# Turned copies of the tokens from the host, split at once; the reciprocal root mean square applied behind the input projection

## The reference, cut to what matters

```python
def rms_norm(x, w):
    y = x * lax.rsqrt(jnp.mean(x * x, axis=-1, keepdims=True) + NORM_EPS)
    return y * w

h = rms_norm(x, norm1_w)                  # 512 x 1024
y = jnp.einsum("bsd,dn->bsn", h, w_in)    # w_in 1024 x 3852
fq, fk, fv, ff, rq, rk, rv, rg, gq, gk, gv, gz, ga, gb = split_columns(y)
qkv = concat([gq, gk, gv])                # 3 x 512 columns
qkv = silu(causal_depthwise_conv(qkv, gdn_conv_w))     # 4 taps along the tokens
# then: attention with forget gates (f*), retention (r*), gated delta rule (g*), w_out,
# a second norm, routed experts, a last norm
```

## Time and profile before

| what | us |
|---|---|
| median of 3 runs | 621.25 (620.01 to 622.05) |
| the profiled execution, its own time | 619.92 |
| its span in the trace | 618.0 |
| PE busy | 579.1 (94% of the span) |
| DVE / ACT / POOL busy | 245.6 / 198.6 / 179.8 |
| first matmul of the projection | at 11.78 |
| first matmul of granule 4 (group v0) | at 37.91 |
| first matmul of granule 16 (group rq) | at 109.99 |

### The profile page before, as it was taken

One profiled execution on the slowest core, in us unless ns is written; L12 is line 12 of the kernel. 1 busy time (PEld: TensorE's weight loads), 2 busy tenths in 40 slices (PEclk: granted clock), 3 DMA queues, 4 the chain that ended last, 5 costly groups with the idle time before them and its releaser, 6 DMA issues.

```text
span 618.0 us, 12011 instructions
## 1 busy us (share of the span) xinstructions
PE 579.1 (94%) x4922; PEld 446.4 (72%) x4922; DVE 245.6 (40%) x618; ACT 198.6 (32%) x429; POOL 179.8 (29%) x118
## 2 busy tenths in 40 slices
PE   7999999999999999999899999999999999987892
PEld 5987887799999888856679998666555565654440
DVE  6135553592216711287732146323332233321117
ACT  7344544523324261634635321111111121111113
POOL 1443434173268422421433301111112111120014
PEclk9999999999999999999999999999999999999997
DMA  9665443422121122003788878999999999999975
GB/s 338 202 187 157 146 134 97 134 70 51 56 70 36 37 69 70 1 2 122 271 325 305 318 265 313 357 421 423 428 422 427 423 429 423 423 425 428 419 299 229
DMA packets 44857, 150.63 MB, mean 244 GB/s; under 512 B 8552, under 2 KB 29760, under 8 KB 38274
## 3 DMA queue, kind: packets, MB, share of 16 engines
q1 hardware_dynamic: 40208, 141.67, 60.4%
q0 software_dynamic: 4528, 8.15, 3.6%
q10 hardware_dynamic: 66, 0.03, 0.0%
HBM read 141.69 MB, written 16.27 MB: 256 GB/s over the span
## 4 chain that ended last, share of the span: by engine, by line
PE 62%; DMA 19%; DVE 11%; issue 4%; ACT 2%; POOL 1%; SPq 0%; DVEq 0%; POOLq 0%; ACTq 0%
PE bank L772 29%; PE bank L796 9%; DMA xg<-h2d,tok 8%; DMA w<-in_expert_w_dram 8%; PE bank L1184 5%; PE bank L1138 4%; PE bank L1160 3%; PE bank L1084 2%; PE bank L1098 2%; DMA yd<-oy,dst 2%; DMA yt<-yd 1%; DVE Dm L1801 1%; PE bank L1078 1%; PE bank L1054 1%; DMA raw<-in_w_in_dram 1%
## 5 line engine op out<-in xcount | busy, mean ns | idle before, releaser
L1506 POOL TENSOR_TENSOR wlo<-raw,whi 128x1024 fp32r<-128x1024 f32 (+1 forms) x25 | 59.9, 2400 | 95.7 <-ACT whi L1207 95.7
L772 PE MATMUL bank<-wlo,hHi 128*128 128x256 f32 (+2 forms) x224 | 64.9, 290 | 0.0
L1138 PE MATMUL bank<-w,xT 128*64 128x256 f32 x512 | 58.2, 380 | 5.1 <-issue 5.1
L772 PE MATMUL bank<-whi,hHi 128*128 128x256 f32 (+1 forms) x208 | 59.9, 288 | 3.2 <-DVE cacc L1701 1.4
L1611 POOL DMA_INDIRECT yd<-oy,dst x15 | 15.1, 1009 | 162.7 <-DVE oy L2140 162.7
L1160 PE MATMUL bank<-w,xT 128*64 128x256 f32 x512 | 58.2, 380 | 2.6 <-DMA w<-in_expert_w_dram 2.6
L1184 PE MATMUL bank<-w,hidT 128*64 128x512 f32 x256 | 58.5, 599 | 1.1 <-ACT hidT L1483 1.1
L1138 PEld LDWEIGHTS bank<-w,xT 128*64 128x64 f32 x512 | 37.8, 137 | 29.4 <-issue 14.5
L772 PE MATMUL bank<-whi,hLo 128*128 128x256 f32 (+1 forms) x208 | 58.7, 282 | 0.0
L1160 PEld LDWEIGHTS bank<-w,xT 128*64 128x64 f32 x512 | 36.4, 137 | 21.5 <-DMA w<-in_expert_w_dram 3.5
L2123 DVE SCALAR_TENSOR_TENSOR hid<-bank,slot,sa 128x256 f32<-128x256 f32 x16 | 10.8, 676 | 94.6 <-issue 92.1
(11 more groups left out here) (374 smaller groups left out, 1121.2 us busy)
## 6 DMA issues: line engine op xcount, KB each, us to landing
w<-in_expert_w_dram SPq DMA_DIRECT2D x44, 2048.0 KB, 21.5
raw<-in_w_in_dram SPq DMA_DIRECT2D x24, 512.0 KB, 3.9
w<-in_expert_w_dram SPq DMA_DIRECT2D x8, 1024.0 KB, 7.1
yd<-zt SPq DMA_DIRECT2D x8, 512.0 KB, 5.1
yt<-yd SPq DMA_DIRECT2D x4, 1024.0 KB, 9.0
raw<-in_w_in_dram SPq DMA_DIRECT2D x6, 520.0 KB, 7.2
X<-in_x_dram SPq DMA_DIRECT2D x4, 512.0 KB, 5.8
raw<-in_w_out_dram SPq DMA_DIRECT2D x4, 512.0 KB, 3.3
```

What stands on the lines that cost most here:

```text
L772: m = pe.matmul(o, l, r, start=(at == 0 and c == 0 and i == 0), stop=(at == parts - 1 and kc == chunks[-1] and i == 2), skip_group_check=True)
L1138: m = pe.matmul(pb[3][r, 0:FF], xT[:, c, r], w1[u % 4][:, e, c * FF:(c + 1) * FF], start=(c == 0), stop=(c == KC - 1), skip_group_check=True)
L1506: pool.tensor_tensor(low_of(g), raw_of(g), high_of(g).bitcast(F32), ALU.subtract).then_inc(wlo_done, 1)
```

## The change

The host sends, beside x, a turned copy of it (`turned`, 128 partitions by 8 chunks by 512 tokens) and one small table `lead` with the norm's weights and the convolution's taps, both laid out by partition. The turned tokens are split at once: ScalarE's high part is a copy with the norm's weight as its scale, chunk by chunk (8 operations of 128x512), VectorE's low part multiplies and subtracts in one operation per chunk. The reciprocal root mean square is taken beside this (ScalarE squares tiles 0 and 1, VectorE tiles 2 and 3) and applied to the projection's outputs: as ScalarE's scale in the "n" groups, and in the "t" groups as a product with `RB`, a table of it along the tokens, which a new task "rb" behind granule 3 makes with four matmuls on TensorE and a copy on VectorE. In the convolution VectorE writes this product into a buffer `yr` in SBUF, which releases the bank; all four taps then read `yr`. fq and fk are evacuated by VectorE instead of ScalarE. TensorE no longer turns tokens; it runs 36 matmuls on zeros first, and runs granule 0 chunk by chunk over four open tiles. The low part of granule 0's weights is shared between VectorE and GpSimd.

```diff
-            tokens(0)
-            tokens(1)
-            sp.dma_start(CT[:, 0:NSTAY], consts[:, 0:NSTAY]).then_inc(s_const, 16)
+            def turned_tokens(i):
+                sp.dma_start(xt0[:, 2 * i:2 * i + 2, :].rearrange("p c n -> p (c n)"),
+                             turned[:, 2 * i * S:(2 * i + 2) * S]).then_inc(s_xt[min(i, 2)], 16)
...
             granule(0)
-            for t in range(2, T):
-                tokens(t)
-            for g in (1, 2):
-                granule(g)
-            sp.dma_start(CT[:, NSTAY:], consts[:, NSTAY:]).then_inc(s_const2, 16)
+            turned_tokens(0)
+            turned_tokens(1)
+            granule(1)
+            turned_tokens(2)
+            turned_tokens(3)
+            tokens(0)
+            tokens(1)
+            granule(2)
+            tokens(2)
+            tokens(3)
+            sp.dma_start(CT[:, 0:NSTAY], consts[:, 0:NSTAY]).then_inc(s_const, 16)
+            sp.dma_start(CT[:, NSTAY:], consts[:, NSTAY:]).then_inc(s_const, 16)
...
+            def first_granule():
+                n, _, _, chunks, _, w, _ = GRANULES[0]
+                hi, lo = high_of(0), low_of(0)
+                tiles = [begin(("y", n, b)) for b in range(T)]
+                pe.wait_ge(first_low, 1)
+                for c, kc in enumerate(chunks):
+                    pe.wait_ge(xlo_done, kc + 1)
+                    if c == HK // 2:
+                        pe.wait_ge(wlo_done, 1)
+                    for b in range(T):
...
+                if k[0] == "rb":
+                    pe.wait_ge(s_const, 32)
+                    pe.wait_ge(ssx_done, 3)
+                    four(k, lambda t, o: mm(o, rx[:, t:t + 1].broadcast_to([P, P]), ident))
...
+            zb = zt.bitcast(BF16)
+            pe.wait_ge(zero_set, 1)
+            for _ in range(WARM):
+                pe.matmul(pb[7][:, 0:256], zb[:, 0:P], zb[:, 0:256], start=True, stop=True)
...
+            def high_part(c):
+                act.wait_ge(s_xt[min(c // 2, 2)], 16 if c < HK else 32)
+                act.activation(hHi[:, c, :], xt0[:, c, :], ACT.Copy, scale=n1p[:, c:c + 1]).then_inc(hhi_done, 1)
+            weight_high(act, 0)
+            act.wait_ge(s_lead, 16)
+            for c in range(HK):
+                high_part(c)
+            weight_high(act, 1)
+            for c in range(HK, KC):
+                high_part(c)
             squares(0)
             squares(1)
...
+            weight_high(act, 2)
+            act.wait_ge(ssx_done, 1)
+            act.activation(ssx, ssx, ACT.Sqrt, scale=1.0 / D, bias=epsm[:, :]).then_inc(ssx_done, 1)
+            act.wait_ge(ssx_done, 3)
...
-                        cp = lambda dst, src: act.activation(dst, src, ACT.Copy)
+                        cp = lambda dst, src: act.activation(dst, src, ACT.Copy, scale=rx[:, t:t + 1])
...
-                        wait_full(act, name)
+                        act.wait_ge(conv_step, 2 * i + 1)
                         if i >= 2:
                             act.wait_ge(silu_done, i - 1)
-                        act.activation(cacc[i % 2][:, :], psum(name)[:, :], ACT.Copy,
+                        act.activation(cacc[i % 2][:, :], yr[i % 2][:, :], ACT.Copy,
                                        scale=PCW[:, 3, blk:blk + 1]).then_inc(tap0_done, 1)
                     for b in range(2):
                         i = CONVN[what] + b
-                        wait_read(act, ("y", n, b))
+                        act.wait_ge(conv_step, 2 * i + 2)
...
+            hc = slice(0, HK // 2)
+            dve.tensor_tensor(low_of(0)[:, hc, :], raw_of(0)[:, hc, :], high_of(0)[:, hc, :].bitcast(F32),
+                              ALU.subtract).then_inc(first_low, 1)
+            for c in range(KC):
+                dve.wait_ge(hhi_done, c + 1)
+                dve.scalar_tensor_tensor(out=hLo[:, c, :], in0=xt0[:, c, :], scalar=n1p[:, c:c + 1],
+                                         in1=hHi[:, c, :].bitcast(F32), op0=ALU.mult, op1=ALU.subtract).then_inc(xlo_done, 1)
+            for t in (2, 3):
+                dve.wait_ge(s_x[t], 16)
+                j = dve.tensor_tensor_reduce(out=X0[:, t, :], in0=X0[:, t, :], in1=X0[:, t, :], scale=1.0, scalar=0.0,
+                                             op0=ALU.mult, op1=ALU.add, accum_out=ssx[:, t:t + 1])
...
                 for b in range(2):
                     name = ("y", n, b)
                     i = CONVN[what] + b
                     blk = tcol[what] + b
+                    wait_full(dve, name)
+                    release(dve.tensor_tensor(yr[i % 2][:, :], psum(name)[:, :], RB[:, :], ALU.mult), name)
+                    wait_read(dve, name)
+                    dve.sem_inc(conv_step, 1)
                     dve.wait_ge(tap0_done, i + 1)
                     a = cacc[i % 2]
                     for s in (1, 2, 3):
-                        j = dve.scalar_tensor_tensor(out=a[:, s:S], in0=psum(name)[:, 0:S - s],
+                        j = dve.scalar_tensor_tensor(out=a[:, s:S], in0=yr[i % 2][:, 0:S - s],
                                                      scalar=PCW[:, 3 - s, blk:blk + 1], in1=a[:, s:S],
                                                      op0=ALU.mult, op1=ALU.add)
```

More of the change, by code:

```diff
@@ L53 @@
 HB = P // 2
+WARM = 36
 FQ, FK, FV, FFG = 0, 256, 512, 768
@@ L124, in tensor_orders @@
 def tensor_orders():
-    a, b = [("par",), ("nb", 0), ("nb", 1)], [("xT", t, i) for t in range(T) for i in range(2)]
+    a, b = [], []
     for g in range(GR_IN):
@@ L779, in granule @@
                         between(b)
+            def first_granule():
[8 more added lines that the diff above has]
+                    for b in range(T):
+                        tk = slice(b * P, (b + 1) * P)
+                        for i, (l, r) in enumerate(((hHi[:, kc, tk], hi[:, c, :]), (hHi[:, kc, tk], lo[:, c, :]),
+                                                    (hLo[:, kc, tk], hi[:, c, :]))):
+                            m = pe.matmul(tiles[b][:, 0:w], l, r, start=(c == 0 and i == 0), stop=False, skip_group_check=True)
+                m.then_inc(half_used, 1)
             def four(name, f):
@@ L865, in task @@
                         four(("u0", t), lambda h, o: mm(o, Um[i][:, h, :], vb[:, t, h, :]))
[L867 to L883 removed]
+            zb = zt.bitcast(BF16)
+            pe.wait_ge(zero_set, 1)
+            for _ in range(WARM):
+                pe.matmul(pb[7][:, 0:256], zb[:, 0:P], zb[:, 0:256], start=True, stop=True)
             for g in range(GR_IN):
[L885 removed]
+                if g:
+                    granule(g)
+                else:
+                    first_granule()
                 for k in AFTER[g]:
@@ L893, in _ @@
                 four(("rT", i), lambda t, o: pe.transpose(o, src[:, t, (i % 2) * P:(i % 2 + 1) * P], ident))
-            pe.wait_ge(y_copied, 6)
+            pe.wait_ge(y_copied, 4)
+            for n in (GIDX["fq"], GIDX["fk"]):
+                for b in range(2):
+                    wait_read(pe, ("y", n, b))
             def step(k):
@@ L1271, in evac @@
                     act.sem_inc(y_copied, 1) if what not in ("zb", "za", "rg") else act.sem_inc(z_in, 1)
-                elif what in ("fq", "fk"):
-                    for b in range(2):
-                        name = ("y", n, b)
-                        wait_full(act, name)
-                        release(act.activation((fqT if what == "fq" else fkT)[:, b, :], psum(name)[:, :], ACT.Copy), name)
-                    act.wait_ge(free[BANK[name][0]], BANK[name][1] + 1)
-                    act.sem_inc(y_copied, 1)
-                else:
+                elif what in CONVN:
                     for b in range(2):
```

130 lines of the change are left out of this document (43 added, 87 removed).

## The result

The changed kernel takes 627.34 us in the median (625.34 to 628.87, 5 runs) against 621.18 for the kernel before on the same chip (620.01 to 622.05): a ratio of 1.010, interval 1.0070 to 1.0131, so +6.2 us. Forecast were +3.05 us (624.3) and a range up to 627.0. The sign was right, the size was half, and the range ended 0.3 too low. The profiled execution took 625.67 us (span 623.6; before 619.92 and 618.0).

What follows compares the result with a forecast made beforehand. TensorE was taken to bound the kernel; start -1.9, task rb +0.9, convolution stalls +1.4 and q1 +2.65 gave +3.05 us, so 624.3 us against the median of 621.25, with a range from 619.0 to 627.0.

Steps and rivals of the forecast that it cites:

- TensorE bounds, and a shift is carried to the end: Whole kernel: TensorE busy 579.1 of 618.0 us; other engines count only where it waits, early shifts last to the end.
- T: Convolution: the moment a group's second tile b1 is full, 86.4 us for k1 and 109.8 for q1.
- The start, -1.9: Start: granule 3's load lands at 26.6 us, so granule 3 starts at 30.2 instead of 32.1, a gain of 1.9.
- rival (d): Start: SP's queue holds up issues and granule 3 lands 1.5 us later; +4.55, 625.8 us; chance 0.10.
- rb's 0.9: Behind granule 3: the task's four float32 matmuls on TensorE cost 0.9 us, bounds 0.5 and 1.0.
- The zeros: Start: the 36 matmuls on zeros give nothing back, as the granted clock was 1.00 in every window there.
- The port: Convolution: taps with two SBUF operands and GpSimd's low parts block each other for whole instructions, costing 3.4 us.
- rival (a): Convolution: taps and GpSimd's low parts don't block each other; sum -0.35, 620.9 us; chance 0.20.
- The third tap of b1: Convolution, k1: this tap holds the port to 9.8 us after T while GpSimd, ready at 9.2, waits; low part ends at 12.2.
- The stalls up to q1's T: Convolution before q1: TensorE waits 1.1 us for k1, 0.25 and 0.05 for v1 and k0, none elsewhere; together 1.4.
- q1, +2.65: Convolution, q1: b1's square ends at T + 11.05, its sum is copied from T + 11.75 instead of T + 9.1; stall 2.65 us.

Runs made afterwards that it cites:

- e4: The changed kernel with granule 3's load issued ahead of the second constants and the six small loads: 623.95 us, ratio 1.0044 against the kernel before.
- e10: The changed kernel with products in PSUM, both before the taps, granule 3's load early, all sums of squares on ScalarE, no zero matmuls: 616.97 us, ratio 0.9942.
- e1: The changed kernel with the convolution's product written back into the PSUM tile, where taps and `cacc` read it: 625.71 us, ratio 1.0049 against the kernel before.
- e13: The changed kernel with two awaited one-number copies on ScalarE ahead of granule 2n+4's high part, 0.45 us later: 625.67 us, ratio 1.0075 against the kernel before.
- e12: The changed kernel with one one-number copy on ScalarE ahead of granule 2n+4's high part, 0.1 us later: 628.09 us, ratio 1.0118 against the kernel before.

## Why the prediction was right or wrong

- **TensorE bounds, and a shift is carried to the end:** right for the start, and wrong in the convolution, where the chain leaves TensorE for 49 us. I took each group's stall from its own T, as if each began on time. In the ring a delay is handed on to the next group.
- **The start, -1.9:** failed at granule 3's landing. I put it at 5.4 us behind its old time; it came at 27.87, 6.7 behind 21.2. Its load took 13.28 us from the issue, before 9.4, and it was issued 2.8 later: 1.3 of the 1.5 that rival (d) gave it. With high and low part (27.89 to 31.43) granule 3 began at 31.48 for 30.2. With rb's 0.9, which was right, granule 4 moved by +0.26 for -1.0. That the load was what ended last was right, and e4 shows the price: 3.5 us. The scale was ready at 22.2 (forecast 22.0), blocked by GpSimd as forecast.
- **The zeros:** that they give nothing back against before holds; granule 0's products follow one another at 0.12 in both the earlier trace rows. The reason that I gave doesn't: the column of the granted clock can't tell, since it reads 1.00 in e10 too, where without any work ahead of them these products run at about half the pace.
- **The port:** right, and rival (a) fell. The first taps behind a low part lasted 2.4 (the forecast's mark was 0.75 or 2.7), those that read PSUM never stretched, in e1 too.
- **The third tap of b1:** the step that failed in the convolution. I had GpSimd ready 0.16 us behind the start of that tap and let it wait. In the trace it came 0.06 ahead, and the tap waited 2.14. That put the SiLU, the next high part and the next `cacc` late, group after group. The stalls up to q1's T hardly show it: +1.4 was forecast, and T came 1.43 later than before, 0.26 of it from the start, so 1.2. That this came out near the forecast is luck, since the order at the port was not the one assumed.
- **q1, +2.65:** here the ring shows. From q1's T to the copy of its second sum it took 9.12 us before (109.8 to 118.92) and 13.84 after (111.23 to 125.07): +4.7. I had ScalarE start q1's high part at T; it was still busy with q0, whose third tap had been blocked, and started at 113.20, T + 2.0. So b0's taps ended at T + 7.6 for T + 5.9, and the last square at T + 12.7 for T + 11.05. In e13, where the third taps are free, the same stretch takes 12.0 (111.71 to 123.71), +2.9: with the order that I had assumed, the term comes out.
- **Not on this path:** TensorE's wait for the copy of k's sums (1.4, forecast at nothing), its waits for q1's banks (1.9, before 1.4, forecast as before), and the lower clock behind them. They delay TensorE ahead of a square that ends last anyway.
- **The sum:** the misses are +1.26 at the start, -0.23 in the stalls and +2.07 at q1, together 3.1, which with the forecast's 3.05 is the 6.15 at q1's copy. Between the profiled executions 5.75 of it are left (625.67 - 619.92), and the medians lie 1.7 and 1.3 above these: 6.2.
- **The range:** it was made of rivals that were mostly cheaper than the forecast. No rival had the convolution becoming the bound, although I had written that VectorE and ScalarE have little to spare.

The Trainium skill, "SBUF — State Buffer", section "SBUF: two separate sides", has it that whichever operation starts first gets the pair for the whole instruction. The whole instruction is what the trace shows (low parts of 2.40, taps of 2.9). Who starts first can't be read off the records: in e12 the tap's record starts 0.04 earlier and the tap waits.

## What to carry to other kernels

When a change adds an operation to an engine beside the bound, add up the ring through the queues (tap, SiLU, high part, `cacc`, tap), with its blocked operations, and compare its period with the bounding engine's; a stall worked out for one group is too small as soon as the period is the longer one. Where two engines contend for a resource within 0.2 us, take both orders as cases with prices. Put the short operations that free banks and feed another engine ahead of a long chain: that order alone took back 5.2 of 6.2 us here, and an operand in PSUM instead of SBUF 3.2. And before you price a wait or a lower clock, look whether the chain runs through it: TensorE's longest waits around q1 cost nothing here, because a square on ScalarE ended later still.

## What the runs showed of the hardware that was not expected

- GpSimd gets the shared port between two VectorE operations that are linked by a semaphore. It got it when it asked 0.06 us before the third tap's start and 0.04 after it, and not 0.4 after it (e13). The same 2.4 us low part delays a tap by 2.1 to 2.2 us or is itself delayed by 0.2 to 0.4.
- `cacc` taps with one operand in PSUM take 746 to 751 ns beside a low part (e1), those with two in SBUF up to 2893 in the changed kernel.
- The time to landing of granule 3's load grew from 9.4 to 13.3 us with 2.1 MB of turned tokens more ahead of it. Issued ahead of the second constants (e4, at 9.2), it still took 12.7, but TensorE never waited for it.
- The granted clock fell behind an idle time of 2.6 us in one execution and didn't behind 2.5 in another.
- Without any product ahead of them, the first products of granule 0 (e10) took 0.42 us each, 0.22 apart, and from 12 us on 0.28, 0.12 apart, while the profile's column of the granted clock read 1.00 throughout.
